# Writing the low part of streamed weights over the tile as loaded: four places shared, four high parts

## The chip, the cores and the metric

The kernel runs on one core of one Trainium2 chip, as one launch. The metric is the device time of an execution in microseconds. The runs shown are three of the kernel before: 1989.61, 1990.55 and 1991.17 us, median 1990.55 us.

## The reference

Two small models run one after the other, with two layers each; all of it is float32, batch 1, 256 tokens, width 1024. The first has an even layer (differential attention and a gated recurrence side by side), an odd layer (three dilated attention branches), and after each a feed-forward with a squared ReLU, layer norms, and a gate by a per-layer embedding. The second modulates its norms by conditions, mixes a gated linear attention, a neighbourhood attention and a windowed attention over 256 context and 256 new tokens, and has a SwiGLU feed-forward. Cut to the shape of the work:

```python
for l in range(2):                                   # first model
    mix = even_mixer(...) if l % 2 == 0 else odd_mixer(...)
    x = layer_norm(ALPHA * x + mix, ...)
    x = layer_norm(ALPHA * x + square(relu(x @ ffn_w1[l])) @ ffn_w2[l], ...)
    x = x + sigmoid(x @ ple_w_gate[l]) * rms_norm(p[l] @ ple_w_proj[l], ...)
...                                                  # second model
    x = x + gate * (concat(gla, near, windowed) @ w_out_2[l])
    x = x + gate * ((silu(h @ w_gate_2[l]) * (h @ w_up_2[l])) @ w_down_2[l])
```

Nearly all of the arithmetic and all of the traffic are products of a few hundred tokens with weights that are read once.

## The kernel before

**Weights.** All weight matrices are cut into blocks of 128 x 128, in the order in which TensorE uses them, and stand in DRAM as one stream of tiles of eight blocks (`TB = 8`), 128 x 1024 float32, 512 KB each. 410 of these are "main" tiles; 96 more hold the weights of the modulations. SyncE loads a main tile into one of four places of `ring` (L370, in `sync_tiles`) and a modulation tile into one of four places of `ring_mod` (L384). Both are issued on SyncE's queue, in one order.

**High and low part.** A product runs in three passes over a reduced float32 format: high part of the weights by high part of x, high by low, low by high (L429, L430 and L431 in `products`; L458, L459 and L460 in `rows_product`, where the weights are the moving side). ScalarE makes the high part by a cast from `ring` to `high` (L396, in `scalar_high`), VectorE the low part by a subtraction, `ring` minus `high`, to `low` (L404, in `vector_low`). There are four places (`RING`) of `ring` and four (`SPLIT`) of `high` and of `low`: twelve tiles of 4 KB a partition. A tile is "used" when the last matmul on its eighth block is done.

**The waits of tile j.** Its load waits for the subtraction of tile j-4 (L367), its cast for tile j-4 to be used (L394) and for its own load (L395), its subtraction for its cast (L403), and TensorE's first block of it for its subtraction (L415).

**Order.** Each engine runs its instructions in a fixed order. A planner lays it out while the program is built (`Program.run`): every piece of work is a generator that yields the name of what it needs; marks give the time at which each thing is expected, a load's with 3.3 us (`later=3.3`, L371); of the pieces that are ready the one of lowest rank goes first. The cast and the subtraction have rank -1 where fewer than two tiles are cast and not yet used, and 2, behind nearly everything, where there are more (`ahead` in `emit`). TensorE takes attention, recurrence and norms (rank 0) before weight products (1) and these before the products of the modulations (3, L546), which so fill gaps.

**Around the products.** ScalarE copies a product out of one of two PSUM banks (L890, L1084 with the ReLU); then come, in the feed-forward, the square L1093, the cast L1106 and the low part L1117. Where a norm of the second model follows, the residual is L1541, the square L1561 (ScalarE), the running sum of squares L1572 (VectorE), its mean over the features L1583 (TensorE), logarithm and exponential L626 and L629 (ScalarE), and then for each block of features L1503, L1525 and L1511, whose result is what the next product waits for.

Of the kernel before, what the change touches and what calls it, by code (L numbers as in the profile page):

```python
# [9 lines left out]
F32 = mybir.dt.float32  # L10
F32R = mybir.dt.float32r
# [5 lines left out]
P = 128  # L17
# [86 lines left out]
TB = 8  # L104
RING = 4
SPLIT = 4
# [84 lines left out]
def V_us(n):  # L191
    return 0.15 + n / 960.0
# [6 lines left out]
class Program:  # L199
    def __init__(self, nc, ctx, io):  # L200
# [29 lines left out]

        sb = lambda scope, name, *shape, dt=F32: scope.enter_context(nc.sbuf_tensor(name, [P, *shape], dt))
        own = lambda name, *shape, dt=F32: sb(ctx, name, *shape, dt=dt)
        self.ring = own("ring", RING, TB * P)
        self.high, self.low = own("high", SPLIT, TB * P, dt=F32R), own("low", SPLIT, TB * P, dt=F32R)
        self.X, self.XH, self.XL = own("X", DC, T2), own("XH", DC, T2, dt=F32R), own("XL", DC, T2, dt=F32R)
        self.SQ, self.RS, self.TMP = own("SQ", 2, 512), own("RS", 2, 512), own("TMP", 4, SEQ)
        self.par, self.wa2 = own("par", NPAR), own("wa2", 256)
# [107 lines left out]
def sync_loads(k):  # L345
    nc, io, D_ = k.nc, k.io, k.D
    for i, half in enumerate((slice(0, DC // 2), slice(DC // 2, DC))):
        nc.sync.dma_start(k.X[:, half, SEQS], io["x"][:, half]).then_inc(
            *D_.tick(k.s_xload[i], 0.1, ("x loaded", i), by=16, later=5.0))
    k.add(D_, sync_tiles(k), 0)  # L350
    yield None
    for buffer, name in [(k.par, "params")] + [(k.c[n], n) for n in GLOBAL_CONSTS + ROPE_CONSTS + ["causal"]]:
        nc.sync.dma_start(buffer[:, :], io[name]).then_inc(
            *D_.tick(k.s_start, 0.1, ("loaded", name), by=16, later=4.0))
        yield None
    k.marks["constants"] = D_.last
    nc.sync.dma_start(k.X[:, :, 0:CTX], io["ctx"]).then_inc(
        *D_.tick(k.s_ctx, 0.1, ("ctx loaded",), by=16, later=9.0))
    k.add(D_, sync_mod_tiles(k), 1)


def sync_tiles(k):

    nc, D_ = k.nc, k.D
    for j in range(k.n_tiles["main"]):
        if j >= RING:
            D_.wait_ge(k.s_low_, (yield "low", j - RING))  # L367
        else:
            yield None
        nc.sync.dma_start(k.ring[:, j % RING, :], k.io["stream"][len(k.order)]).then_inc(  # L370
            *D_.tick(k.s_raw[j % RING], 0.1, ("raw", j), by=16, later=3.3))  # L371
        D_.clock += 1.3
        k.order.append(("main", j))
# [26 lines left out]
def vector_low(k):  # L400
    nc, V = k.nc, k.V
    for j in range(k.n_tiles["main"]):
        V.wait_ge(k.s_high, (yield "high", j))  # L403
        nc.vector.tensor_tensor(k.low[:, j % SPLIT, :], k.ring[:, j % RING, :], k.high[:, j % SPLIT, :].bitcast(F32),  # L404
                                ALU.subtract).then_inc(*V.tick(k.s_low_, V_us(TB * P), ("low", j)))


def weights(k, blocks):

    stream = k.stream["main"]  # L410
    tile, o = len(stream) // TB, len(stream) % TB
    stream += blocks
    assert o + len(blocks) <= TB
    if o == 0:
        k.T.wait_ge(k.s_low_, (yield "low", tile))  # L415
    s = slice(o * P, (o + len(blocks)) * P)
    used = [("used", tile)] if o + len(blocks) == TB else []
    return k.high[:, tile % SPLIT, s], k.low[:, tile % SPLIT, s], used


def products(k, names, outs, columns, ks, moving):

    nc, T = k.nc, k.T
    for i, c in enumerate(ks):
        for key, out, (name, layer, col) in zip(names, outs, columns):
            wh, wl, used = yield from weights(k, [(name, layer, c, col)])
            xh, xl = yield from moving(c)
            n = xh.shape[1]
            nc.tensor.matmul(out, wh, xh, start=(i == 0), stop=False)  # L429
            nc.tensor.matmul(out, wh, xl, start=False, stop=False)  # L430
            m = nc.tensor.matmul(out, wl, xh, start=False, stop=(c == ks[-1]))  # L431
            if c == ks[-1]:
                m.then_inc(*T.tick(k.s_products, 3 * T_us(n), key, *used))
            elif used:
                m.then_inc(*T.tick(k.s_used, 3 * T_us(n), *used))
            else:
                T.spend(3 * T_us(n))
            yield None
# [8 lines left out]
def rows_product(k, keys, frees, name, layer, cols, stationary):  # L447

    nc, T = k.nc, k.T
    banks, w = [], P * len(cols)  # L450
    for i, (key, free) in enumerate(zip(keys, frees)):
        k.bank_of[key] = yield from k.banks["gemm" if i < 2 else "small"].take(T, free)
        banks.append(k.bank[k.bank_of[key]])
    for c in range(DC):
        wh, wl, used = yield from weights(k, [(name, layer, c, col) for col in cols])
        for i, bank in enumerate(banks):
            xh, xl = yield from stationary(c, i)
            nc.tensor.matmul(bank[:, 0:w], xh, wh, start=(c == 0), stop=False)  # L458
            nc.tensor.matmul(bank[:, 0:w], xl, wh, start=False, stop=False)  # L459
            m = nc.tensor.matmul(bank[:, 0:w], xh, wl, start=False, stop=(c == DC - 1))  # L460
            mine = used if i == len(banks) - 1 else []
            if c == DC - 1:
                m.then_inc(*T.tick(k.s_products, 3 * T_us(w), keys[i], *mine))
            elif mine:
                m.then_inc(*T.tick(k.s_used, 3 * T_us(w), *mine))
            else:
                T.spend(3 * T_us(w))
            yield None
# [1649 lines left out]
def emit(k):  # L2118
# [8 lines left out]
    k.add(T, tensor_context_norm(k), 2)  # L2127
    k.add(A, scalar_high(k), ahead)
    k.add(V, vector_low(k), ahead)
    k.add(A, x_high(k), 0)  # L2130
    k.add(V, x_low(k), 0)
# [311 lines left out]
```

## Time and profile before

| | |
|---|---|
| median of three runs | 1990.55 us |
| the profiled execution | 1993.38 us, span of its instructions 1992.1 us |
| mean granted TensorE clock | 0.972 |
| TensorE busy | 1874.0 us, 94% |
| VectorE busy | 1096.3 us, 55%; the 410 subtractions 502.4 us of it |
| ScalarE busy | 885.6 us, 44%; the 410 casts 428.1 us of it |
| traffic | 276.88 MB, mean 139 GB/s |

Busy times are of the engines, not of their sequencers; matmuls are pipelined, so one that is said to last 327 ns may be followed by the next after 120. "Idle before" is the time that an engine stood still just ahead of an instruction, and the name behind the arrow is what ended it.

### The profile page before, as it was taken

The numbers are of one execution on the slowest core, as the hardware profiler recorded it, in microseconds if no ns is written. First come the engines' busy times: TensorE is split into PE (matmuls) and PEld (weight loads), VectorE is DVE, ScalarE is ACT, GpSimd is POOL, SyncE is SP. The second block draws the span as 40 slices with busy tenths as digits, with TensorE's granted clock in tenths as the row PEclk, the third lists the DMA queues.
The fourth block names the chain that finished last, engine by engine and source line by source line (L and its number), as shares of the span: only waits on it lengthen the run. The fifth ranks groups of instructions, "written<-read, shape, count | busy, mean of one in ns | idle before, by whom it ended". The sixth has DMA issues, their size and how long they took to land. (4 is left out here: it accounts for less than half of the span.)

```text
span 1992.1 us, 29858 instructions
## 1 busy us (share of the span) xinstructions
PE 1874.0 (94%) x12320; PEld 1583.5 (79%) x12320; DVE 1096.3 (55%) x1971; ACT 885.6 (44%) x1495; POOL 94.2 (5%) x92
## 2 busy tenths in 40 slices
PE   6988999999999999889999989999999799979998
PEld 5956899978868999677775668888888687569998
DVE  5556656566756565646546663333334575555554
ACT  4554545355435453655434442222232664444443
POOL 0000100040001000310101000000000001100000
PEclk9989999999999999898999989999999899989999
DMA  7477655575366555331220022222322222124553
GB/s 267 162 250 267 218 184 184 191 263 202 104 236 230 185 181 183 131 111 46 75 85 22 23 73 95 99 94 94 104 96 96 74 75 85 53 85 161 185 184 107
DMA packets 79624, 276.88 MB, mean 139 GB/s; under 512 B 9200, under 2 KB 13168, under 8 KB 79488
## 3 DMA queue, kind: packets, MB, share of 16 engines
q1 hardware_dynamic: 77840, 269.66, 39.9%
q0 software_dynamic: 1648, 5.31, 0.9%
q8 instruction: 98, 1.61, 0.3%
q14 instruction: 38, 0.31, 0.1%
HBM read 273.88 MB, written 1.05 MB: 138 GB/s over the span
## 5 line engine op out<-in xcount | busy, mean ns | idle before, releaser
L404 DVE TENSOR_TENSOR low<-ring,high 128x1024 fp32r<-128x1024 f32 x410 | 502.4, 1227 | 436.2 <-ACT high L396 434.9
L429 PE MATMUL bank<-XH,high 128*128 128x256 f32 (+1 forms) x2096 | 684.4, 327 | 60.8 <-DVE XL L1511 21.8
L430 PE MATMUL bank<-XL,high 128*128 128x256 f32 (+1 forms) x2096 | 666.0, 318 | 0.0
L431 PE MATMUL bank<-XH,low 128*128 128x256 f32 (+1 forms) x2096 | 665.1, 317 | 0.0
L396 ACT CAST high<-ring 128x1024 fp32r<-128x1024 f32 x410 | 428.1, 1045 | 471.8 <-PE bank L431 418.8
L429 PEld LDWEIGHTS bank<-XH,high 128*128 128x128 f32 x2096 | 406.5, 194 | 117.0 <-DVE XL L1511 27.4
L430 PEld LDWEIGHTS bank<-XL,high 128*128 128x128 f32 x2096 | 407.7, 195 | 23.8 <-issue 0.2
L431 PEld LDWEIGHTS bank<-XH,low 128*128 128x128 f32 x2096 | 407.0, 194 | 24.6
L431 PE MATMUL bank<-hidden_high,low 128*128 128x256 f32 (+1 forms) x864 | 264.6, 306 | 0.0
L430 PE MATMUL bank<-hidden_low,high 128*128 128x256 f32 (+1 forms) x864 | 264.1, 306 | 0.0
L429 PE MATMUL bank<-hidden_high,high 128*128 128x256 f32 (+1 forms) x864 | 261.9, 303 | 0.0
L429 PEld LDWEIGHTS bank<-hidden_high,high 128*128 128x128 f32 x864 | 163.9, 190 | 8.0
L430 PEld LDWEIGHTS bank<-hidden_low,high 128*128 128x128 f32 x864 | 161.7, 187 | 8.5
L431 PEld LDWEIGHTS bank<-hidden_high,low 128*128 128x128 f32 x864 | 162.2, 188 | 7.6
L546 PE MATMUL bank<-ring_mod,conditions 128*32 128x256 f32 x768 | 62.4, 423 | 21.9 <-DMA ring_mod<-in_stream 21.8
L2010 ACT ACTIVATE TMP<-bank 128x512 f32<-128x512 f32 (+1 forms) x44 | 21.6, 491 | 116.5 <-PE bank L431 116.5
L820 ACT ACTIVATE mix_scores<-mix_scores,small 128x512 f32<-128x512 f32 (+1 forms) x72 | 46.5, 647 | 58.2 <-DVE small L752 57.9
L458 PE MATMUL bank<-high,XH 128*128 128x512 f32 (+1 forms) x192 | 70.1, 365 | 2.2 <-ACT gk L890 1.5
L459 PE MATMUL bank<-high,XL 128*128 128x512 f32 (+1 forms) x192 | 68.0, 354 | 0.0
L460 PE MATMUL bank<-low,XH 128*128 128x512 f32 (+1 forms) x192 | 68.0, 354 | 0.0
L1541 DVE SCALAR_TENSOR_TENSOR X<-bank,mod,X 128x256 f32<-128x256 f32 x72 | 32.6, 480 | 61.6 <-PE bank L431 61.6
L1084 ACT ACTIVATE TMP<-bank 128x256 f32<-128x256 f32 x64 | 24.5, 384 | 83.1 <-PE bank L431 80.5
(304 smaller groups left out, 1934.4 us busy)
## 6 DMA issues: line engine op xcount, KB each, us to landing
ring<-in_stream SPq DMA_DIRECT2D x410, 512.0 KB, 3.2
ring_mod<-in_stream SPq DMA_DIRECT2D x96, 512.0 KB, 5.5
nb<-in_rpb POOLq DMA_DIRECT2D x12, 256.0 KB, 3.2
X<-in_x SPq DMA_DIRECT2D x2, 512.0 KB, 4.0
X<-in_ctx SPq DMA_DIRECT2D x1, 1024.0 KB, 7.4
out<-y SPq DMA_DIRECT2D x8, 128.0 KB, 2.0
pT<-in_p POOLq DMA_DIRECT2D x2, 256.0 KB, 6.3
c_window<-in_window POOLq DMA_DIRECT2D x1, 512.0 KB, 4.3
```

The lines of the kernel that those rows point to most:

```text
L396: nc.scalar.copy(k.high[:, j % SPLIT, :], k.ring[:, j % RING, :]).then_inc(*A.tick(k.s_high, A_us(TB * P), ("high", j)))
L404: nc.vector.tensor_tensor(k.low[:, j % SPLIT, :], k.ring[:, j % RING, :], k.high[:, j % SPLIT, :].bitcast(F32), ALU.subtract).then_inc(*V. ...
L429: nc.tensor.matmul(out, wh, xh, start=(i == 0), stop=False)
L430: nc.tensor.matmul(out, wh, xl, start=False, stop=False)
L431: m = nc.tensor.matmul(out, wl, xh, start=False, stop=(c == ks[-1]))
L458: nc.tensor.matmul(bank[:, 0:w], xh, wh, start=(c == 0), stop=False)
L459: nc.tensor.matmul(bank[:, 0:w], xl, wh, start=False, stop=False)
L460: m = nc.tensor.matmul(bank[:, 0:w], xh, wl, start=False, stop=(c == DC - 1))
L546: m = nc.tensor.matmul(k.bank[b][32 * j:32 * j + 32, 0:256], k.cs[:, c, :], raw[:, 256 * j:256 * j + 256], start=(c == 0), stop=(c == DC - 1),
L820: nc.scalar.activation(T_[:, to:to + cols], T_[:, to:to + cols], ACT.Exp, bias=nm[:, j:j + 1], scale=-1.0, accum_out=den[:, j:j + 1]).then ...
L1084: nc.scalar.activation(k.TMP[:, j, :], k.bank[k.bank_of[tag, "product", i]][:, 0:SEQ], ACT.Relu).then_inc(*A.tick(k.s_copied, A_us(SEQ), ( ...
L1541: nc.vector.scalar_tensor_tensor(k.X[:, i, s], bank[:, side * CTX - lo:(side + 1) * CTX - lo], k.mod[:, layer, gate + i, side:side + 1], k ...
```

## The change

The buffer `low` has four places and lies over `ring`: the ring's memory is given back as soon as it is laid out, and `low`, asked for next, gets the same addresses. The subtraction of tile j so writes its result over the tile that it reads. A place is then in use until TensorE has used the low part, and the load of tile j waits for tile j-4 to be used. `high` keeps its four places. Eight tiles of 4 KB a partition stand where twelve stood. The cast, its waits, the subtraction's waits and the counts (`RING = 4`, `SPLIT = 4`, `TB = 8`) are as before.

```diff
-        self.ring = own("ring", RING, TB * P)
-        self.high, self.low = own("high", SPLIT, TB * P, dt=F32R), own("low", SPLIT, TB * P, dt=F32R)
+
+        with ExitStack() as t:
+            self.ring = sb(t, "ring", RING, TB * P)
+        self.low, self.high = own("low", RING, TB * P, dt=F32R), own("high", SPLIT, TB * P, dt=F32R)
...
         if j >= RING:
-            D_.wait_ge(k.s_low_, (yield "low", j - RING))
+            D_.wait_for((yield "used", j - RING))
...
-        nc.vector.tensor_tensor(k.low[:, j % SPLIT, :], k.ring[:, j % RING, :], k.high[:, j % SPLIT, :].bitcast(F32),
+        nc.vector.tensor_tensor(k.low[:, j % RING, :], k.ring[:, j % RING, :], k.high[:, j % SPLIT, :].bitcast(F32),
...
-    return k.high[:, tile % SPLIT, s], k.low[:, tile % SPLIT, s], used
+    return k.high[:, tile % SPLIT, s], k.low[:, tile % RING, s], used
```

## Rows read from the trace of the kernel before

**Rows 1.** The page: busy times, then groups (line, engine, form | busy, mean ns | idle before).
```profile
PE 1874.0 (94%) x12320; PEld 1583.5 (79%) x12320; DVE 1096.3 (55%) x1971; ACT 885.6 (44%) x1495; POOL 94.2 (5%) x92
...
L404 DVE TENSOR_TENSOR low<-ring,high 128x1024 fp32r<-128x1024 f32 x410 | 502.4, 1227 | 436.2 <-ACT high L396 434.9
...
L396 ACT CAST high<-ring 128x1024 fp32r<-128x1024 f32 x410 | 428.1, 1045 | 471.8 <-PE bank L431 418.8
```

**Rows 2.** Waits, all engines: who waited for whom, us in total, times, longest.
```profile
DVE low L404 <- ACT high L396: 434.9, 332, 6.2
ACT high L396 <- PE bank L431: 418.8, 183, 4.6
...
PEld bank L546 <- DMA ring_mod<-in_stream: 31.2, 23, 3.2
...
PEld bank L429 <- DVE low L404: 19.0, 1, 19.0
```

**Rows 3.** Waits of SyncE's queue; then the modulation loads, first and last start.
```profile
SPq L370 <- DVE low L404: 1647.2, 406, 95.4
SPq L384 <- PE bank L546: 125.4, 67, 6.5
...
L384 SPq DMA_DIRECT2D ring_mod<-in_stream x96: 327/328/1246, 11.0 to 803.7; - x96
```

**Rows 4.** Windows: busy us of each engine (instructions), granted clock, DMA share, GB/s.
```profile
240.00:380.00 140.00, 140.00 (x1169) 140.00 (x1168) 83.54 (x111) 64.04 (x93) 0.00 (x0) 1.00 0.54 183
1800.00:1940.00 140.00, 140.00 (x1169) 140.00 (x1168) 77.04 (x95) 61.12 (x86) 0.00 (x0) 1.00 0.54 181
1200.00:1500.00 300.00, 300.00 (x1315) 246.48 (x1315) 102.85 (x118) 80.09 (x99) 0.00 (x0) 1.00 0.29 97
```

**Rows 5.** Groups of VectorE by form: an output of its own, and one over an input.
```profile
L1117 DVE TENSOR_TENSOR hidden_low<-TMP,hidden_high 128x512 fp32r<-128x512 f32 x22 | 15.1, 685 | 0.0
...
L1704 DVE TENSOR_TENSOR gla_k_out<-gla_k_out,gk 128x512 f32<-128x512 f32 x8 | 5.5, 691 | 8.7 <-ACT gk L890 6.4 <-ACT gla_k_out L1739 2.3
```

**Rows 6.** Ring loads: page (median landing); the line's stretches 680:712 and 449:453.
```profile
ring<-in_stream SPq DMA_DIRECT2D x410, 512.0 KB, 3.2
...
L370 SPq DMA_DIRECT2D ring<-in_stream x12: 327/328/328, 679.8 to 711.8; - x12
...
DMA to landing us min/median/max: 3.3/4.2/4.3
...
L370 SPq DMA_DIRECT2D ring<-in_stream x2: 327/328/328, 450.3 to 452.1; - x2
...
DMA to landing us min/median/max: 5.9/6.1/6.4
```

**Rows 7.** Timeline (start, us, engine, line) of ScalarE and VectorE, feed-forward.
```profile
243.28 1.04 ACT L396 CAST high<-ring 128x1024 fp32r<-128x1024 f32 x1
...
245.88 0.38 ACT L1084 ACTIVATE TMP<-bank 128x256 f32<-128x256 f32 x1 [1.26 <-PE bank L431]
...
243.42 0.42 DVE L1093 TENSOR_TENSOR TMP<-TMP 128x256 f32<-128x256 f32 x1 [0.38 <-ACT TMP L1084]
244.35 1.23 DVE L404 TENSOR_TENSOR low<-ring,high 128x1024 fp32r<-128x1024 f32 x1 [0.51 <-ACT high L396]
```

**Rows 8.** Timeline at three norms: 1782 us, 1983 us (the last), 1544 us.
```profile
1782.32 1.23 DVE L404 TENSOR_TENSOR low<-ring,high 128x1024 fp32r<-128x1024 f32 x1 [0.59 <-ACT high L396]
...
1784.03 1.19 PE L1583 MATMUL bank<-RS,c_meanD 128*128 128x256 f32 x2 [2.82 <-DVE RS L1572]
...
1984.50 0.70 PE L1583 MATMUL bank<-RS,c_meanD 128*128 128x256 f32 x2 [1.49 <-DVE RS L1572]
...
1545.48 0.62 ACT L1561 ACTIVATE SQ<-X 128x512 f32<-128x512 f32 x1
...
1546.74 0.68 DVE L1572 TENSOR_TENSOR RS<-RS,SQ 128x512 f32<-128x512 f32 x1
...
1547.57 1.19 PE L1583 MATMUL bank<-RS,c_meanD 128*128 128x512 f32 x2 [3.09 <-DVE RS L1572]
```

## The prediction

> **What bounds the kernel now.** I read the page first. TensorE is busy for 1874.0 of 1992.1 us, VectorE for 1096.3 and ScalarE for 885.6 [rows 1], so a change pays only through what TensorE waits for. The change touches the road of the weights, so next I read the waits. TensorE waited for a low part once, for 19.0 us, and that is the start of the kernel; behind it no row has it waiting for L404 or L396. The long waits run the other way: ScalarE stands idle for 418.8 us before its casts, until TensorE has used a tile, and VectorE 434.9 us before its subtractions until the cast is done [rows 2]. SyncE waits 1647.2 us for L404 before its loads [rows 3]. So the weights are early everywhere, and the loop that holds them back is "high part used, cast, subtract". Lastly the windows: in three stretches, 580 us together, TensorE has no gap. In two of them it runs 1169 matmuls in 140 us; 24 of these use up a tile, so a tile lasts 24 x 140 / 1169 = 2.87 us. In the third, 1315 in 300 us, with twice the columns, a tile lasts 5.48 us [rows 4]. These are the two paces that a load must keep up with. Counted through the matmuls of the whole trace, some 200 of the 410 tiles go at the fast pace.
>
> **What changes: the write in place.** No instruction is added or removed: 410 casts of 1045 ns, 410 subtractions of 1227 ns [rows 1] and 410 loads stay. VectorE now writes over an input. Nearest rows: L1704, which writes over its first input, takes 691 ns at 512 elements, L1117, which doesn't, 685 [rows 5]. So 0 to 1%, at most 5 us of VectorE's 502, on an engine that is idle 45% of the time and under matmuls: I take 0. The buffers behind move down by 16 KB a partition; no row gives that a price, and I take nothing.
>
> **What moves is the load.** Before, load j follows the subtraction of tile j-4; from now on it follows the last matmul on it. The cast of tile j waits for "used j-4" in both kernels; in the new one the landing lies between the two. The new loop: handover to SyncE 0.05 us, landing 3.2 us [rows 6], cast 1.04, subtraction 1.23, and two or three handovers of 0.03 us (the cast of 243.28 ends at 244.32, its subtraction starts at 244.35 [rows 7]): 0.05 + 3.2 + 1.04 + 1.23 + 0.1, some **5.7 us**. TensorE meanwhile has three tiles ready: 3 x 2.87 = 8.6 us at the fast pace, 16.4 us at the slow one. **The slack is 2.9 us in the one and 10.7 us in the other.** It was 8.6 - 2.7 = 5.9 us (0.3 behind the copy L1084, 1.04, 1.23, handovers), and the load starts 5.9 + 2.9 = 8.8 us later than before. Cost at the median landing: nothing, hidden under three tiles of matmuls; with that cover used up, each further microsecond on a slot's round costs 0.25 us a tile. The phase is good as well: a load at 243.0 lands at 246.2, just behind the copy L1084 of the next product (245.88 [rows 7]), where the next cast stands today; all casts slide by one tile.
>
> **Does the landing stay at 3.2 us?** Not always. Twelve loads in one stretch have a median of 4.2 us [rows 6], with no other load near; that leaves 1.9 us. The loads of the modulation weights (96, up to 803.7 us [rows 3]) are issued in bunches on the same queue; two ring loads behind one took 5.9 and 6.4 us [rows 6], up to 3.2 over the median against 2.9 of slack. I put each load of before, with its own landing, behind the "used" of its time and added the waits that its cast and subtraction had on their engines: 9 of 406 tiles come late, by 6.4 us in sum, most of them behind a bunch; behind one late tile the next finds the queue clear. Between 0 and 6.4 us I take 1.5. The other side of it: at the start of a transition up to four loads of 512 KB fewer stand in the queue that TensorE waits for there (31.2 us on ring_mod [rows 2]). Its bound is a few microseconds won; I take nothing.
>
> **SyncE's queue** is in order. Behind the wait for "used" stand later ring_mod loads, as they stood behind the wait for L404, and TensorE's L546 waits for those; behind the last waits stand the stores of the result, which come after all loads anyway. The reverse, ring loads behind a wait for a used modulation tile (125.4 us over 67 waits, none over 6.5 [rows 3]), was covered by a whole ring of loaded tiles and now is by the 2.9 us alone. The order comes from a planner that counts 3.3 us for a landing, so I expect each load to stand about where it becomes free.
>
> **The transitions, where something may be won.** At the end of a product, cast and subtraction of the slot just freed run at once, ahead of the norm. At 1782.32 us VectorE takes L404 and only then L1572, and TensorE idles 2.82 us before L1583; the same step at the very end, where no tile is left, has a gap of 1.49 us [rows 8]. So the pair costs 1.33 us there. At 1544 us, with 512 columns, the gap is 3.09 us; the square ends at 1546.10, and L1572 starts at 1546.74, behind L404 [rows 8]: 0.6 us, and a like place stands at 1169 us. From now on the pair comes 3.3 us later. At the slow pace that falls into the wait for the rsqrt: won 2 x 0.6. At the fast pace the pair of the tile before moves to about 0.5 us behind the product's end, where the old one stood, and the 1.33 us hang on a tie. Bounds: 2.5 us won, or as much lost where a late pair falls ahead of the first L1503. I take 1.5 us won, by the two like places.
>
> Sum: 0 + 1.5 - 1.5 = 0 us on a profiled execution of 1993.4 us (span 1992.1), which lies 2.8 us over the median of the runs shown: 1990.5, say **1990 us**.
>
> **A rule that speaks against the change.** All of the 3.2 us of landing lies ahead of need today [rows 6]. The Trainium skill, "DMA: Bandwidth & Descriptors", section "Rules for kernel authors", says to issue a DMA early and to wait for it late, so that its fixed cost is overlapped; this change issues each one three tiles later. And the skill's "Perfetto Trace Analysis", section "Optimization Strategy", reads a gap that repeats on the engine that should be full as a sign of too few buffers for the next tile. By that rule the fast stretches would show gaps; the trace of before has none [rows 4], and by the slack above none come. If they do, it is the first rival.
>
> **The rivals.**
> - *The load becomes the bound at the fast pace (slower).* Place: the 200 tiles at 2.87 us. It decides from 2.9 us over the loop's 5.7. Landings of 4.2 use 1.0 of it [rows 6]; the copy L1084 (0.38) on ScalarE and L1093 (0.42) on VectorE [rows 7], with as much again for the copies L1106 and L1117 beside them, can stand in front of a late cast or subtraction, 1.6 us in all. At 3.1 us over, it costs 0.05 x 200 = 10 us; at 4 us over, 55 us. For it: the engines run in a fixed order, and a cast that waits for its landing also holds the copy that frees one of TensorE's banks. Against it: nearly all must meet at once, and the bunches end at 804 us. Price +12 us, 2002 us; chance 0.23.
> - *The transitions gain more (faster).* The pair's 1.3 us come off at several norms and mixers, and the modulation loads find the queue free: -7 us, 1984 us (five such places); chance 0.14.
> - *The change doesn't do what it says.* If the loads did not move at all, because something else holds them, the time is 1990.5. SyncE's 1647.2 us of waiting for L404 [rows 3] speak against it; it is part of the forecast's case.
>
> **How the numbers follow.** Forecast 0.63, 1987 to 1995 us; slower rival 0.23; faster 0.14. A measurement of this kernel tells from no change what is over about 0.2%, 4 us, and of the forecast's own case 0.02 lies above that: same 0.61, slower 0.25, faster 0.14. Leaving out 2 in 10, the far part of the slower rival and a third of the faster, the range is 1984 to 2003 us.
>
> **What would show it.** Right: L370 released by TensorE and not by L404; ScalarE's idle time before casts ended by a landing; no wait of PE or PEld for L404 beyond the first, and as many matmuls in the fast windows; L404 still at 1227 ns; the gaps at 1169 and 1544 us 0.6 us shorter. Wrong: rows of PEld waiting for L404, fewer matmuls in the fast windows, landings over 5 us without a bunch, ScalarE's copies late behind a cast.

## The result, and the profile after

The changed kernel takes 1999.21 us in the median of seven runs (1994.1 to 2005.14) against 1989.61 us of the kernel before in seven (1984.61 to 1991.17): ratio 1.0054, interval 1.0038 to 1.0069 (a ratio and its interval come from all runs of a series; the medians alone give 1.0048). That is slower by half a percent, on the side of the first rival. Eleven further runs, beside 23 of before on one chip, gave 1.0034 (1.0020 to 1.0048). The forecast was 1990 us, the range ended at 2003.

From L237 on, the lines of the changed kernel stand two lower: the cast is L398, the subtraction L406, the loads L372 and L386, the passes L431 to L433. First the page of the changed kernel: busy times, the chain that ended last, and the two groups.

```profile
PE 1874.2 (94%) x12320; PEld 1582.9 (79%) x12320; DVE 1088.6 (55%) x1971; ACT 902.2 (45%) x1497; POOL 79.7 (4%) x92
...
PE 84%; ACT 5%; DMA 5%; DVE 4%; issue 1%; SPq 0%; ACTq 0%; DVEq 0%
PE bank L431 23%; PE bank L432 22%; PE bank L433 22%; PE bank L723 3%; PE bank L690 3%; DMA ring<-in_stream 3%; DMA ring_mod<-in_stream 2%; PE bank L705 2%; PE bank L548 2%; PE bank L460 1%; PE bank L462 1%; PE bank L461 1%; ACT high L398 1%; PE bank L863 1%; ACT L628 1%
...
L406 DVE TENSOR_TENSOR low<-ring,high 128x1024 fp32r<-128x1024 f32 x410 | 502.3, 1227 | 564.0 <-ACT high L398 562.9
...
L398 ACT CAST high<-ring 128x1024 fp32r<-128x1024 f32 x410 | 429.2, 1047 | 580.7 <-DMA ring<-in_stream 578.6
```

The subtraction lasts 1227 ns in place, as it did with a buffer of its own [rows 1]. The busy time of TensorE is the same. What is new is who ends the idle time before a cast: a landing (the end of a load), where it was TensorE [rows 2]. And loads of the weight stream stand in the chain that ended last, with 3% of the span. The page of the kernel before can't be set beside that, since its chain covers only 21% of the span; the kernel with the same order and early loads, further down, lists no such entry in a chain of 99%. The waits (who waited for whom, us in total, times, longest) and the windows of the stretches without a gap:

```profile
ACT high L398 <- DMA ring<-in_stream: 578.6, 290, 13.6
...
PEld bank L431 <- DVE low L406: 22.1, 3, 18.4
...
240.00:380.00 140.00, 140.00 (x1169) 140.00 (x1168) 81.48 (x111) 64.76 (x91) 0.00 (x0) 1.00 0.57 183
...
1200.00:1500.00 300.00, 300.00 (x1315) 246.58 (x1314) 100.88 (x114) 84.64 (x99) 0.00 (x0) 1.00 0.29 97
```

TensorE still waits for a low part at the start (18.4 us) and else for 3.7 us in two places, as much as with the same order and early loads. Its pace in the full stretches (those in which it has no gap) is unchanged to the matmul, 1169 and 1315 [rows 4]. So the loads are no bound where weights are used fastest, and yet the kernel is slower. SyncE's queue does what the change says, released by TensorE:

```profile
SPq L372 <- PE bank L433: 1570.5, 378, 94.2
```

The profiled execution has a span of 1995.5 us, 3.4 over that of before; single executions lie up to 0.3% from the medians of these series, and up to 0.4% in later ones, so for the size of an effect I read the medians of many runs, and the traces for the place.

### The profile page after: what moved, and what is told of

It reads as the page before. It is cut to its first block, busy times and chain, and to the rows that moved or that the text cites. A ratio compares the mean times of both kernels' runs of the same rounds, so it can differ in the third digit from the quotient of the medians.

```text
span 1995.5 us, 29827 instructions
## 1 busy us (share of the span) xinstructions
PE 1874.2 (94%) x12320; PEld 1582.9 (79%) x12320; DVE 1088.6 (55%) x1971; ACT 902.2 (45%) x1497; POOL 79.7 (4%) x92
## 4 chain that ended last, share of the span: by engine, by line
PE 84%; ACT 5%; DMA 5%; DVE 4%; issue 1%; SPq 0%; ACTq 0%; DVEq 0%
PE bank L431 23%; PE bank L432 22%; PE bank L433 22%; PE bank L723 3%; PE bank L690 3%; DMA ring<-in_stream 3%; DMA ring_mod<-in_stream 2%; PE bank L705 2%; PE bank L548 2%; PE bank L460 1%; PE bank L462 1%; PE bank L461 1%; ACT high L398 1%; PE bank L863 1%; ACT L628 1%
## 5 line engine op out<-in xcount | busy, mean ns | idle before, releaser
L406 DVE TENSOR_TENSOR low<-ring,high 128x1024 fp32r<-128x1024 f32 x410 | 502.3, 1227 | 564.0 <-ACT high L398 562.9
L431 PE MATMUL bank<-XH,high 128*128 128x256 f32 (+1 forms) x2096 | 683.5, 326 | 65.9 <-DVE XL L1513 26.0
L398 ACT CAST high<-ring 128x1024 fp32r<-128x1024 f32 x410 | 429.2, 1047 | 580.7 <-DMA ring<-in_stream 578.6
L433 PE MATMUL bank<-XH,low 128*128 128x256 f32 (+1 forms) x2096 | 664.4, 317 | 0.0
L431 PEld LDWEIGHTS bank<-XH,high 128*128 128x128 f32 x2096 | 405.7, 194 | 119.8 <-DVE XL L1513 30.5
L433 PEld LDWEIGHTS bank<-XH,low 128*128 128x128 f32 x2096 | 406.2, 194 | 24.4
L433 PE MATMUL bank<-hidden_high,low 128*128 128x256 f32 (+1 forms) x864 | 264.6, 306 | 0.0
L431 PE MATMUL bank<-hidden_high,high 128*128 128x256 f32 (+1 forms) x864 | 261.9, 303 | 0.0
L431 PEld LDWEIGHTS bank<-hidden_high,high 128*128 128x128 f32 x864 | 163.9, 190 | 8.0
L433 PEld LDWEIGHTS bank<-hidden_high,low 128*128 128x128 f32 x864 | 162.2, 188 | 7.5
L1108 ACT CAST hidden_high<-TMP 128x256 fp32r<-128x256 f32 (+1 forms) x108 | 48.0, 446 | 47.1 <-DVE TMP L2027 43.8
L1119 DVE TENSOR_TENSOR hidden_low<-TMP,hidden_high 128x256 fp32r<-128x256 f32 (+1 forms) x108 | 51.1, 475 | 17.3 <-ACT hidden_high L1108 17.3
L723 PE MATMUL bank<-mix_turned,v 128*64 128x256 f32 x240 | 58.2, 390 | 0.0
```

What stands on the lines that cost most here:

```text
L398: nc.scalar.copy(k.high[:, j % SPLIT, :], k.ring[:, j % RING, :]).then_inc(*A.tick(k.s_high, A_us(TB * P), ("high", j)))
L406: nc.vector.tensor_tensor(k.low[:, j % RING, :], k.ring[:, j % RING, :], k.high[:, j % SPLIT, :].bitcast(F32), ALU.subtract).then_inc(*V.t ...
L723: m = nc.tensor.matmul(out[:, q0:SEQ], u["v"](kt), PTi[:, kt, q0:SEQ], start=(kt == 0), stop=(kt == keys - 1))
L1119: nc.vector.tensor_tensor(hl[:, i % half, :], k.TMP[:, j:j + w, :].rearrange("p a t -> p (a t)"), hh[:, i % half, :].bitcast(F32), ALU.sub ...
```

## The experiments

Three theories. LATE: landings that take longer than the slack make TensorE wait for weights. ORDER: the planner, told of the new wait, lays out other orders on all engines, and those cost the time. PLACE: the write in place, or the moved buffers. After the first four runs a sharper form of LATE took the lead, HELD: a late cast costs TensorE nothing by its own tile; it stands at the head of ScalarE's queue, and what stands behind it is late.

**Once more, and with twelve places.** The changed kernel again:

> The changed kernel once more, for a narrower interval and a second profile. Every theory: 0.3 to 0.8% slower than before (1995 to 2005 us). Theory LATE (some executions have landings that take longer than the 2.9 us of slack, and TensorE waits for weights then): a second profile may show waits of PEld for the low part L406 behind the first, and a longer span goes with them. Theory ORDER (the planner's other order costs the time, loads are never late): such waits stay at 3 and under 4 us beside the start, and the gla stage of layer 1 (1590 to 1660 us) is again the place of 4 to 6 us.

Then the same orders and waits, but with buffers as before:

```diff
-        with ExitStack() as t:
-            self.ring = sb(t, "ring", RING, TB * P)
-        self.low, self.high = own("low", RING, TB * P, dt=F32R), own("high", SPLIT, TB * P, dt=F32R)
+        self.ring = own("ring", RING, TB * P)
+        self.high = own("high", SPLIT, TB * P, dt=F32R)
+        self.low = own("low", RING, TB * P, dt=F32R)
```

> The load of tile j waits for tile j-4 to be used, as in the changed kernel, and every engine has the changed kernel's order; but ring, high and low have twelve places of their own, as before. Theories LATE and ORDER: as slow as the changed kernel, ratio 1.004 to 1.007. Theory PLACE (writing over the tile, or the buffers moved down 16 KB, costs the time): 1.000 to 1.002.

Measured 1.0034 (1.0020 to 1.0048) and 1.0029 (1.0016 to 1.0043). The second lies under what LATE and ORDER expected and over what PLACE did. It is slower than before with no write in place and no buffer moved, so PLACE falls as the cause of the loss; a share of 1 or 2 us these runs can't tell from nothing. In the second profile of the changed kernel TensorE's waits for the low part are again three, 24.0 us with 20.3 at the start, so the simple form of LATE gets no support either.

**The new order with early loads.** On top of the twelve places, one line: the planner is told of the new wait, the queue waits for the old one. All five engines have the instructions of the changed kernel in its order; in the traces the sequences of operations and buffers are the same to the last instruction, so a gap can be compared by the number of its matmul.

```diff
-            D_.wait_for((yield "used", j - RING))
+            D_.wait_ge(k.s_low_, [(yield "used", j - RING), k.marks["low", j - RING]][1])
```

> Every engine has the changed kernel's order (the planner is told that a load waits for the used tile), but the load really waits for the subtraction of tile j-4 alone, in buffers of their own, as before. Theory LATE: the loss goes, 1.000 to 1.002 at most. Theory ORDER: the loss stays, 1.004 to 1.007 (+8 to +14 us).

Measured 0.9967 (0.9955 to 0.9979), 1984.63 us: not only did the loss go, it is faster than before. Beside it, on the same chip, the one that differs only in the wait took 1996.83 us. **The change is thus two effects of opposite sign: the order gives some 6 us, the late loads take 12.** They leave the 6 to 7 us of this series; the first series had 9.6. ORDER, as a theory of the loss, falls.

**The old order with late loads.** The reverse can be made only for part of the tiles: with the order of before and all loads late, the queue would stand behind a wait for a tile that TensorE can't reach without a modulation tile queued behind it. From tile 216 on there are none (the counts are those of the used marks, written into a table; `USED` holds them):

```diff
-            D_.wait_ge(k.s_low_, (yield "low", j - RING))
+            m = yield "low", j - RING
+            t = USED[j - RING]
+            D_.wait_for(m if j < 216 else Mark(k.s_products if t[0] == "p" else k.s_used, int(t[1:]), 0.0))
```

> The order of every engine is that of the kernel before, buffers too; only from tile 216 on (811 us) the load of tile j waits for tile j-4 to be used. That is 194 of 406 loads and about 70 of the 200 tiles at the fast pace. Theory LATE: a third of the loss or more, +3 to +6 us, ratio 1.0015 to 1.003, and waits of PEld for L404 in the windows 1800 to 1950 us. Theory ORDER: no loss, 0.999 to 1.001.

Measured 1.0444 (1.0426 to 1.0462), 88 us slower: far outside what either theory said, and of the sign of LATE. Its lines stand two lower again. The waits from 816 us on, the window 1880 to 2030, and ScalarE's timeline in it:

```profile
ACT high L400 <- DMA ring<-in_stream: 530.4, 188, 6.2
...
1880.00:2030.00 150.00, 142.22 (x1145) 139.39 (x1145) 73.69 (x93) 60.88 (x84) 0.00 (x0) 0.99 0.49 166
...
1964.67 1.05 ACT L400 CAST high<-ring 128x1024 fp32r<-128x1024 f32 x1 [1.96 <-DMA ring<-in_stream]
...
1970.70 1.05 ACT L400 CAST high<-ring 128x1024 fp32r<-128x1024 f32 x1 [2.35 <-DMA ring<-in_stream]
1971.65 0.38 ACT L2014 ACTIVATE TMP<-bank 128x256 f32<-128x256 f32 x1
```

The casts wait a few us each for their landing, and the copy L2014, which frees one of TensorE's banks, starts in the moment that the cast ends: it had been standing behind it. The order of before has the cast ahead of the copy, which is right for a tile that has landed and wrong for one that lands 3 us later. TensorE is busy for 142.22 of 150 us, in a kind of stretch that had no gap [rows 4]. It still doesn't wait for a low part there; it waits most often (8 times) for VectorE's L2029, the multiplication that reads this copy. From this picture HELD was formed.

**The same in the changed kernel.** The two kernels of one order, the changed one and the one with early loads, can be laid side by side. At the norm near 1170 us, the changed kernel, ScalarE and then TensorE (start, us, engine, line; in brackets the idle time before and its releaser):

```profile
1170.04 0.63 ACT L1563 ACTIVATE SQ<-X 128x512 f32<-128x512 f32 x1 [2.13 <-DVE X L1543]
1172.18 1.04 ACT L398 CAST high<-ring 128x1024 fp32r<-128x1024 f32 x1 [1.51 <-DMA ring<-in_stream]
1173.24 1.28 ACT L628 ACT_TABLE_LOAD   x1
1174.53 0.69 ACT L628 ACTIVATE RS<-bank,c_cols 128x512 f32<-128x512 f32 x1
...
1168.51 0.39 PE L433 MATMUL bank<-XH,low 128*128 128x512 f32 x1
1171.54 1.10 PE L1585 MATMUL bank<-RS,c_meanD 128*128 128x512 f32 x2 [2.64 <-DVE RS L1574]
1179.71 0.80 PE L431 MATMUL bank<-XH,high 128*128 128x512 f32 x1 [7.08 <-DVE XL L1513]
```

The same place with early loads:

```profile
1159.19 0.63 ACT L1563 ACTIVATE SQ<-X 128x512 f32<-128x512 f32 x1 [3.87 <-PE bank L433]
1159.72 1.03 ACT L398 CAST high<-ring 128x1024 fp32r<-128x1024 f32 x1
1160.77 1.28 ACT L628 ACT_TABLE_LOAD   x1
1162.11 0.69 ACT L628 ACTIVATE RS<-bank,c_cols 128x512 f32<-128x512 f32 x1
...
1157.80 0.39 PE L433 MATMUL bank<-XH,low 128*128 128x512 f32 x1
1160.69 1.38 PE L1585 MATMUL bank<-RS,c_meanD 128*128 128x512 f32 x2 [2.50 <-DVE RS L1574]
1167.29 0.79 PE L431 MATMUL bank<-XH,high 128*128 128x512 f32 x1 [5.22 <-DVE XL L1513]
```

The order is the same: square, cast, table load, logarithm. With the tile there, the cast runs in the shadow of the norm's first matmuls (1159.72, before their 1160.69). Late, it stands idle for 1.51 us, starts 0.64 us behind them, and the table load and the logarithm L628 of the norm follow it. From L1585 to L628 it is 2.99 us against 1.42, and TensorE waits 7.08 us for the normalised columns against 5.22. From the product's last matmul to the first of the next it is 11.20 us against 9.49; in the kernel before (1168.73 to 1178.71, single execution) it was 9.98. So the gap ahead of L1585 did get shorter, 2.64 us against 3.09 [rows 8], and one line further more than that is given back. The late load had no part in what was won: with early loads in this order the gap is 2.50 us.

A second place, in the product that follows, the changed kernel and then early loads:

```profile
1191.40 1.05 ACT L398 CAST high<-ring 128x1024 fp32r<-128x1024 f32 x1 [2.09 <-DMA ring<-in_stream]
1192.47 1.28 ACT L2012 ACT_TABLE_LOAD   x1
1193.76 0.60 ACT L2012 ACTIVATE TMP<-bank 128x512 f32<-128x512 f32 x1
...
1194.41 0.50 PE L431 MATMUL bank<-XH,high 128*128 128x512 f32 x1 [1.99 <-ACT TMP L2012]
```

```profile
1176.96 1.04 ACT L398 CAST high<-ring 128x1024 fp32r<-128x1024 f32 x1
1178.02 1.28 ACT L2012 ACT_TABLE_LOAD   x1
1179.85 0.60 ACT L2012 ACTIVATE TMP<-bank 128x512 f32<-128x512 f32 x1 [0.55 <-PE bank L433]
```

Here the copy waits for nothing of its own; it is only behind the cast, and TensorE, which needs its bank, stands 1.99 us. With early loads the copy waits for TensorE, as it should, and TensorE not at all. A third is the norm at the fast pace, near 1788 us. The changed kernel, then early loads:

```profile
1785.20 1.04 ACT L398 CAST high<-ring 128x1024 fp32r<-128x1024 f32 x1 [1.41 <-DMA ring<-in_stream]
1786.15 0.41 ACT L1563 ACTIVATE SQ<-X 128x256 f32<-128x256 f32 x1
...
1788.09 1.04 ACT L398 CAST high<-ring 128x1024 fp32r<-128x1024 f32 x1 [1.52 <-DMA ring<-in_stream]
...
1794.40 0.58 PE L431 MATMUL bank<-XH,high 128*128 128x256 f32 x1 [5.23 <-DVE XL L1513]
```

```profile
1767.53 0.42 ACT L1563 ACTIVATE SQ<-X 128x256 f32<-128x256 f32 x1 [1.52 <-DVE X L1543]
1767.85 1.03 ACT L398 CAST high<-ring 128x1024 fp32r<-128x1024 f32 x1
...
1774.63 0.58 PE L431 MATMUL bank<-XH,high 128*128 128x256 f32 x1 [4.00 <-DVE XL L1513]
```

One late cast holds the square L1563, so that TensorE idles 3.23 us ahead of L1585 instead of 2.47; the next holds the logarithm, and it idles 5.23 us ahead of L431 instead of 4.00. The three places make 1.9, 2.0 and 2.0 us, and they repeat: all four profiled executions in this order whose loads are late outside the full stretches have them within 0.3 us, and none of the five others has (both groups stand in the table below). One more gap of this pair doesn't: at 622 us TensorE stood 1.32 us for a copy L1086 behind a late cast, but the other three had 0.07 us there or nothing, so it is an accident of one execution.

**One place more.** Two theories of how much slack is wanted stood beside HELD's bare form: BUNCH, that only loads behind a bunch of modulation loads are too late, so all is lost before 810 us; and PACE, that the tiles at the fast pace cost it. With five places, and with six, in place as before and with the order of the changed kernel, a load waits for the use of tile j-5 or j-6:

```diff
-RING = 4
+RING = 5
-        if j >= RING:
-            D_.wait_for((yield "used", j - RING))
+        if j >= SPLIT:
+            D_.wait_for([(yield "used", j - SPLIT), k.marks["used", j - RING] if j >= RING else k.marks["low", 0]][1])
```

> Written in place as in the changed kernel, and every engine has the changed kernel's order; but with five places, so that the load of tile j waits for tile j-5 to be used, one tile earlier (2.9 us at the fast pace, 5.5 at the slow one). Theory HELD (a cast whose tile has not landed stands at the head of ScalarE's queue and holds the copies, logarithms and casts of x behind it; the time is lost at norms and in the mixers, not at the fast pace): the larger part of the 12 us between the changed kernel and the same order with early loads goes: ratio to before 0.997 to 1.000, and ScalarE's idle time before casts, ended by a landing, falls from 579 us to under 200. Rival BUNCH (what the new order costs late loads is the modulation loads' bunches alone): only what is lost before 810 us can go, about half, 0.999 to 1.001.

> As the one with five places, but six: the load of tile j waits for tile j-6, two tiles earlier than in the changed kernel, 5.7 us at the fast pace, more than a landing takes. Theory HELD: as fast as the same order with the load right behind the subtraction: 0.996 to 0.998, faster than before, with ten tiles of memory instead of twelve. If instead the write in place itself costs anything, it stays above the 0.9967 of the early loads by that.

Measured 0.9979 (0.9970 to 0.9987) and 0.9981 (0.9970 to 0.9992). Both are faster than before; the loss is gone with one place more. Their subtractions still write in place and their buffers are moved. They stand 0.0006 to 0.0014 over the two series with early loads and buffers as before (0.9967, and 0.9973 below), that is 1 to 3 us, with intervals that overlap: no more than that is left for PLACE. ScalarE's idle time before casts, as far as a landing ended it, with five places and then with six:

```profile
ACT high L398 <- DMA ring<-in_stream: 185.4, 98, 12.6
...
ACT high L398 <- DMA ring<-in_stream: 51.3, 20, 13.0
```

So 98 casts still wait with five places, and against six it costs nothing that can be measured (1984.66 and 1984.36 us). And BUNCH falls: of the 11.6 us between the spans of the changed kernel and of six places, 6.0 lie ahead of the matmul that starts at 806 us in the changed kernel and 5.6 behind it, where no modulation load is. Over all nine profiled executions of this order the two groups named above differ by 7.0 us ahead of that matmul and by 6.6 behind it.

**A plan with longer landings.** The planner counts 3.3 us for a landing. If it is told 4.3, it should put the casts later and let the copies pass:

```diff
-            *D_.tick(k.s_raw[j % RING], 0.1, ("raw", j), by=16, later=3.3))
+            *D_.tick(k.s_raw[j % RING], 0.1, ("raw", j), by=16, later=4.3))
```

> The changed kernel, but the planner counts 4.3 us for a landing of a main tile instead of 3.3 (L373), so that casts stand one microsecond later in every engine's order. Theory HELD: fewer casts stand at the head of ScalarE's queue before their tile is there; a part of the loss goes, 1.000 to 1.003, if the slack of 2.9 us bears one more. Rival LATE at the fast pace: worse, 1.006 or more, with waits of PEld for the low part.

Beside it the same order with early loads and twelve places:

> The order of the kernel that plans 4.3 us for a landing, but with the loads really waiting for the subtraction of tile j-4 alone, in twelve places. Against that one it gives the price of the late loads in another order: theory HELD expects 0.3 to 0.6% between the two again. Against the early loads in the 3.3 us order it tells how much of that one's gain of 0.33% is luck of one order: if casts that come later in the order are better in themselves, 0.995 to 0.997; if it was luck, 0.999 to 1.001.

Measured 1.0099 (1.0082 to 1.0115) and 1.0027 (1.0014 to 1.0040). That missed what HELD expected of the first: it is slower, not faster. It is as slow as the rival LATE said, but without its sign: TensorE waits for a low part once, 17.1 us at the start. The second missed too; both of its ranges ended at 1.001. The pair tells why the bare number was no test: the new plan is a third order, and with early loads alone it is 0.27% slower than before. Between the two, in one order, the late loads cost 0.72%, over the 0.3 to 0.6% expected and at the least as much as in the changed kernel's order. A planner told of a longer landing does not mend it. In this order the norm at 1170 us has 6.35 us ahead of L431 in both. The norm at the fast pace (near 1800 us) loses as above: 3.27 us against 2.47 ahead of L1585, 5.06 against 4.00 ahead of L431.

**Which tiles.** In the order of the changed kernel, with its twelve places, 211 loads were made late that lie in the stretches without a gap, and the rest early; then the other way round; and all early once more, on the same chip:

```diff
-            D_.wait_for((yield "used", j - RING))
+            used = yield "used", j - RING
+            late = 46 <= j < 100 or 152 <= j < 204 or 256 <= j < 311 or 354 <= j < 404
+            D_.wait_for(used if late else k.marks["low", j - RING])
```

> The changed kernel's order, twelve places. The load waits for the used tile only for the 211 tiles whose loads fall into the stretches in which TensorE has no gap (tiles 46-99, 152-203, 256-310, 354-403); the other 195 loads wait for the subtraction, as before. Theory HELD (late casts cost time only where ScalarE also has the work on which TensorE waits, at norms, attention and mixers): as fast as with all loads early, 0.996 to 0.998. Rival PACE (the loads are the bound at the fast pace, as the prediction's first rival had it): as slow as the changed kernel, 1.002 to 1.005.

> The complement: the same order and places, the 211 loads of the steady stretches early and the other 195 late. Theory HELD: as slow as the changed kernel, 1.002 to 1.005. Rival PACE: 0.996 to 0.998.

> All loads early in the changed kernel's order, once more, beside the two that split the late loads. All theories: 0.9955 to 0.998, faster than before; the two splits are read against this one.

Measured 0.9982 (0.9966 to 0.9997), 1.0029 (1.0013 to 1.0045) and 0.9973 (0.9959 to 0.9988): medians of 1984.88, 1996.18 and 1984.32 us. **The 195 loads outside the full stretches cost 11.9 us, the 211 in them 0.6 us by the medians and 1.8 by the means, which can't be told from nothing.** PACE falls. The waits of ScalarE for landings, first with the 211 late, then with the 195:

```profile
ACT high L400 <- DMA ring<-in_stream: 389.8, 196, 14.4
...
ACT high L400 <- DMA ring<-in_stream: 249.1, 122, 14.9
```

The kernel that waits longer in sum is the one that loses nothing. In a full stretch of this order a late cast finds ScalarE with nothing queued behind that TensorE wants soon; at a norm and at the end of a product it does. That is no property of the stretch: in the order of before, late loads took TensorE to 142.22 of 150 us in one.

TensorE's idle time (span less busy time of the page) goes the same way, and so does the wait for L1513 at the norm near 1170 us (L1515 in the two that split the loads), both from one profiled execution each. The medians are from different chips, so the ratio to the kernel before, measured beside each, is given too; the first row is that of the three runs shown at the start:

| kernel | median us | ratio | TensorE idle us | wait at the norm us |
|---|---|---|---|---|
| before | 1990.55 | 1 | 118.1 | 5.22 |
| changed | 1999.21 | 1.0054 | 121.3 | 7.08 |
| changed, again | 1997.97 | 1.0034 | 123.8 | 7.17 |
| twelve places, all late | 1996.83 | 1.0029 | 123.6 | 7.18 |
| 195 others late | 1996.18 | 1.0029 | 121.5 | 7.17 |
| 211 late in full stretches | 1984.88 | 0.9982 | 113.3 | 5.22 |
| all early | 1984.63 | 0.9967 | 111.3 | 5.22 |
| all early, again | 1984.32 | 0.9973 | 113.5 | 5.46 |
| five places | 1984.66 | 0.9979 | 112.3 | 5.46 |
| six places | 1984.36 | 0.9981 | 111.5 | 5.22 |

Within the order of the changed kernel, the four with late loads outside the full stretches idle 7.8 to 12.5 us more than the five without: most of the 12 us that the medians differ by. Of a mean of 10.2 us, 6.3 lie behind the matmul at 806 us, and the three places above make most of those. Ahead of it 3.9 us are spread over small gaps that differ from execution to execution, 1.4 of them at the very start, where no load waits for a used tile.

**Is the order's gain a rule?** A third order, from a plan with 2.3 us a landing, all loads early, twelve places:

```diff
-            *D_.tick(k.s_raw[j % RING], 0.1, ("raw", j), by=16, later=3.3))
+            *D_.tick(k.s_raw[j % RING], 0.1, ("raw", j), by=16, later=2.3))
```

> Loads early, twelve places, but the planner counts 2.3 us for a landing and the used tile before it: a third order. The order planned with 3.3 us was 0.33% faster than before, the one with 4.3 us 0.27% slower. Theory LUCK (such differences are the chance of one order, not the later place of the casts): anywhere from 0.996 to 1.004. Rival PLACE OF THE CAST (a later cast is better, as the prediction had it for the norms): between before and the 3.3 us order, 0.997 to 1.000.

Measured 1.0006 (0.9992 to 1.0020). With early loads throughout, the plans for 2.3, 3.3 and 4.3 us give 1.0006, 0.9967 (again: 0.9973) and 1.0027. The gain of 6 us belongs to one order and not to the wait or to a landing planned later; I take it for chance, and three orders are few to say more.

## Why the prediction was wrong

**What bounds the kernel** was right: TensorE at 94%, and no wait of it for a weight but at the start.

**The write in place at nothing** was right as far as can be told: 1227 ns a subtraction in both kernels, 502.3 us in sum against 502.4 [rows 1]. Six places in place (0.9981) beside twelve places with buffers as before (0.9967, 0.9973), where loads aren't late in either, leave 1 to 3 us, inside the intervals.

**The slack at the two paces** was right (the terms of the loop add up to 5.6 us and not 5.7, which changes nothing): 1169 matmuls in 240 to 380 us and 1315 in 1200 to 1500 as before [rows 4], and 211 late loads there for at most 1.8 us, inside the noise. It held even where landings took 4.3 us (below). It held for TensorE's wait on weights and for the order that the planner laid out, not for any order, as the late loads in the order of before show.

**"9 of 406 tiles come late ... I take 1.5", between 0 and 6.4.** This is the step that failed. Within the changed kernel's order the late loads cost 12 us. The count was of tiles that come late for TensorE's use of them, and of these there are next to none. What costs is the cast, an instruction at the head of ScalarE's in-order queue, and what stands behind it: L628 with its table load, L1563, L2012. The prediction had this in words, in the first rival's "a cast that waits for its landing also holds the copy that frees one of TensorE's banks", but placed it at the fast pace, where little comes of it, and took from it nothing for the term. The trace of before gave reason to price it: ScalarE's casts waited for TensorE 183 times [rows 2]; each of these now has a landing, 3.2 us, ahead of it, and the question at each norm is whether the cast stands ahead of the square or the logarithm. It does.

**"At the slow pace that falls into the wait for the rsqrt: won 2 x 0.6".** The size was nearly right and its cause wasn't. The gaps ahead of L1585 are 2.64 us near 1170 and 2.56 near 1547 us against 3.09 [rows 8], 0.45 and 0.53 won:

```profile
1549.02 1.10 PE L1585 MATMUL bank<-RS,c_meanD 128*128 128x512 f32 x2 [2.56 <-DVE RS L1574]
...
1787.98 1.19 PE L1585 MATMUL bank<-RS,c_meanD 128*128 128x256 f32 x2 [3.23 <-DVE RS L1574]
```

But with early loads in the same order both are 2.50 us: the order, with the square ahead of the cast, won them, and not the later landing. At the fast pace the gap grew from 2.82 to 3.23 us, within the bound given; there too the order alone shortened it, to 2.47 us. What failed is "falls into the wait": the cast doesn't wait beside the rsqrt, its table load and logarithm stand behind it on the same engine. I had looked for what the pair leaves and not for what it lands in front of.

**The order at nothing.** "I expect each load to stand about where it becomes free" was right for SyncE's queue (378 + 28 waits, all released by TensorE). But the planner, told of another wait, laid out TensorE, VectorE and ScalarE anew (only SyncE and GpSimd have the sequence of before), and that was worth 6 us in this case, more than the whole forecast of the transitions. I had no term for it; nothing in the trace of before would have given its sign, so it belonged into the range.

**The range** held the time, 1999.21 in 1984 to 2003, since the first rival's price (+12) met the size of the late loads. That was luck: its mechanism at the fast pace was not what happened, and its place wasn't either; the sum came out near by two effects of opposite sign, -6 and +12, neither of which the forecast had.

**The rule against the change**, to issue early and wait late (the Trainium skill, "DMA: Bandwidth & Descriptors", section "Rules for kernel authors"), was borne out: the same order with early loads is 12 us faster. The sign that I looked for by the Trainium skill, "Perfetto Trace Analysis", section "Optimization Strategy", a gap that repeats on the engine that should be full, did not come: the full stretches have none, and the loss stands in single gaps at different steps.

## What stays open

Of the 12 us, three places with 5.8 us are shown row by row, all behind 1100 us; the rest is located only by the split, by halves and by the idle time. Ahead of 806 us, where half of the loss lies, that casts hold other work is argued and not shown: there the late loads share their queue with the modulation loads, and no run keeps the two apart. TensorE's waits for modulation loads at least are no longer in the four executions with late loads outside the full stretches (16.8 to 21.7 us) than in the five others (17.9 to 20.8). That the order's 6 us are chance rests on three orders. A change of the cast's place alone, behind the logarithm, would test HELD at one norm; it was not tried.

## What to carry to other kernels

When a load is moved behind a wait, the first question isn't whether its data come in time for the engine that uses them, but what is queued behind the instruction that waits for it; price that at the transitions, where the order is tight, and not by the slack of the steady pace alone. The sum of an engine's waiting says nothing of its cost: 389.8 us of it were as good as free and 249.1 us cost 12. Where a planner or a scheduler stands between an edit and the order, hold the order fixed and move the wait alone, or two effects are read as one; and one buffer more (five places for four) can be all that the move lacks.

## What the runs showed of the hardware

Landings of 512 KB can lie on another level for a whole full stretch. In 250 to 380 us, 45 loads of the changed kernel, then the same window in its second profile and in the kernel before (median in the last column):

```profile
ring<-in_stream SPq DMA_DIRECT2D x45, 512.0 KB, 4.3
...
ring<-in_stream SPq DMA_DIRECT2D x46, 512.0 KB, 3.3
...
ring<-in_stream SPq DMA_DIRECT2D x45, 512.0 KB, 3.2
```

The first two are one kernel with the same order, so the program doesn't fix the level; what sets it is open. Nor does it last through an execution: from 620 to 780 us the first has 3.3 us and the second 4.3. It had no part in the loss: the kernel with twelve places and all loads late took 3.2 and 3.3 us in these two windows and lost as much. The kernel whose landings were planned at 4.3 had 4.3 us too in the first window, and 3.2 in the second.

A gap on TensorE can be paid for a second time, in the matmuls that follow it. Windows of the changed kernel behind the norm near 1170 us, and behind the wait for the copy at 1194 us (busy us and instructions of each engine, then TensorE's granted clock):

```profile
1179.00:1182.00 3.00, 2.29 (x5) 1.83 (x6) 3.00 (x9) 1.87 (x5) 0.00 (x0) 0.50 0.00 0
1182.90:1186.00 3.10, 3.10 (x15) 2.54 (x14) 3.10 (x9) 1.97 (x5) 0.00 (x0) 0.99 0.00 0
...
1194.40:1197.00 2.60, 2.59 (x11) 2.17 (x12) 1.55 (x3) 1.57 (x2) 0.00 (x0) 1.00 0.25 101
```

After 7.08 us without a matmul the granted clock is at 0.50, 1.2 GHz, and the passes of 512 columns start 0.43 us apart; from 1182.9 us on it is at 2.4 GHz, and they start 0.23 us apart. The slow part lasts 3.2 us there, and 4.0 with early loads (1167.29 to 1171.29), so it is a price of the norm and not of this change. Behind the gap of 1.99 us the granted clock is 1.00: that one was paid once.
